# Moving the squaring of the hidden units and the residual's gain to other places in VectorE's order of an fp32 MLP

## What is computed

```
def squared_relu_mlp(x, w1, w2):
    h = jax.nn.relu(x @ w1)          # (256, 2048) @ (2048, 8192)
    return (h * h) @ w2              # (256, 8192) @ (8192, 2048)

x = layer_norm(ALPHA * x + mix, ln_mix_g[layer], ln_mix_b[layer])
x = layer_norm(ALPHA * x + squared_relu_mlp(x, mlp_w1[layer], mlp_w2[layer]), ln_mlp_g[layer], ln_mlp_b[layer])
```

## Time and profile before

| | |
|---|---|
| time, median of 3 runs | 2160.62 us (2160.14 to 2162.01) |
| the profiled execution: its time, its span | 2162.01 us, 2159.9 us |
| TensorE busy | 2131.8 us, 99% of the span |
| VectorE busy | 1423.9 us, 66% |
| ScalarE busy | 990.5 us, 46% |
| granted TensorE clock, mean | 0.997 |
| chain that ended last, by engine | PE 97%, DVE 1%, DMA 1% |

### The profile page before, as it was taken

How to read it: one execution, slowest core, us unless ns; L and a number is a source line. 1 busy time by engine, 2 the same in 40 slices (tenths; PEclk the granted TensorE clock), 3 DMA queues, 4 the chain that set the end, 5 groups by cost and what they waited for, 6 DMA issues and landing times.

```text
span 2159.9 us, 27393 instructions
## 1 busy us (share of the span) xinstructions
PE 2131.8 (99%) x10034; PEld 1786.6 (83%) x10034; DVE 1423.9 (66%) x1448; ACT 990.5 (46%) x1160; POOL 28.4 (1%) x38
## 2 busy tenths in 40 slices
PE   8999999999999999999999999999999999999997
PEld 7888888888888888888888888888888888888886
DVE  5866766766666666666787666567666666566667
ACT  4545656444444444444645554554444444444442
POOL 2000000000000000000000000000000000000002
PEclk9999999999999999999999999999999999999998
DMA  9554565666666666665564555456666666666662
GB/s 281 176 176 156 174 235 166 225 226 201 204 194 224 204 200 196 216 202 196 186 218 155 191 175 175 176 158 210 224 217 202 201 203 209 204 203 207 201 213 106
DMA packets 244767, 425.83 MB, mean 197 GB/s; under 512 B 14992, under 2 KB 50048, under 8 KB 243696
## 3 DMA queue, kind: packets, MB, share of 16 engines
q1 hardware_dynamic: 242880, 415.75, 59.5%
q0 software_dynamic: 1840, 9.44, 1.3%
HBM read 406.26 MB, written 2.10 MB: 189 GB/s over the span
## 4 chain that ended last, share of the span: by engine, by line
PE 97%; DVE 1%; DMA 1%; ACT 0%; SPq 0%; issue 0%
PE ps L714 26%; PE ps L716 26%; PE ps L715 26%; PE ps L688 11%; PE ps L692 5%; DMA raw<-in_ev_w_in 1%; PE ps L789 0%; PE ps L754 0%; PE ps L830 0%; PE ps L734 0%; PE ps L733 0%; PE ps L732 0%; PE ps L788 0%; PE ps L793 0%; DVE res L1125 0%; DVE stats L1091 0%
## 5 line engine op out<-in xcount | busy, mean ns | idle before, releaser
L380 ACT ACTIVATE w_hi<-raw 128x1024 fp32r<-128x1024 f32 x752 | 794.1, 1060 | 951.0 <-PE ps L716 888.7
L1005 DVE TENSOR_TENSOR w_lo<-raw,w_hi 128x1024 fp32r<-128x1024 f32 x752 | 901.4, 1218 | 302.6 <-ACT w_hi L380 302.4
L714 PE MATMUL ps<-w_hi,yT 128*128 128x512 f32 x1240 | 483.8, 390 | 0.0
L716 PE MATMUL ps<-w_hi,yT 128*128 128x512 f32 x1240 | 482.5, 389 | 0.0
L715 PE MATMUL ps<-w_lo,yT 128*128 128x512 f32 x1240 | 482.4, 389 | 0.0
L714 PE MATMUL ps<-w_hi,xT 128*128 128x512 f32 x1216 | 475.3, 391 | 2.1 <-DVE xT L1035 2.1
L716 PE MATMUL ps<-w_hi,xT 128*128 128x512 f32 x1216 | 473.3, 389 | 0.0
L715 PE MATMUL ps<-w_lo,xT 128*128 128x512 f32 x1216 | 473.2, 389 | 0.0
L1077 DVE TENSOR_TENSOR res<-ps,res 128x1024 f32<-128x1024 f32 x131 | 160.3, 1224 | 225.6 <-PE ps L716 225.6
L715 PEld LDWEIGHTS ps<-w_lo,yT 128*128 128x128 f32 x1240 | 232.8, 188 | 48.2
L716 PEld LDWEIGHTS ps<-w_hi,yT 128*128 128x128 f32 x1240 | 232.8, 188 | 48.3
(11 more groups left out here) (181 smaller groups left out, 775.1 us busy)
## 6 DMA issues: line engine op xcount, KB each, us to landing
raw<-in_mlp_w SPq DMA_DIRECT2D x256, 1024.0 KB, 5.3
raw<-in_od_w_in SPq DMA_DIRECT2D x48, 1024.0 KB, 5.2
raw<-in_ev_w_in SPq DMA_DIRECT2D x36, 1024.0 KB, 5.1
raw<-in_ev_w_out SPq DMA_DIRECT2D x16, 1024.0 KB, 5.1
ks<-cross SPq DMA_DIRECT2D x512, 32.0 KB, 1.9
raw<-in_od_w_out SPq DMA_DIRECT2D x16, 1024.0 KB, 5.0
raw<-in_ev_w_in SPq DMA_DIRECT2D x8, 512.0 KB, 13.1
res<-in_x SPq DMA_DIRECT2D x8, 256.0 KB, 9.7
```

Of the source, the lines that this page charges most:

```text
L380: nc.scalar.activation(flat(w_hi[:, k % NSPL]), flat(raw[:, k % NRAW]), ACT.Copy).then_inc(s_hi, 1)
L714: nc.tensor.matmul(bank, src[:, kt + i, 0, toks], hi, start=(start and i == 0), stop=False)
L716: ins = nc.tensor.matmul(bank, src[:, kt + i, 1, toks], hi, start=False, stop=(stop and i == CK - 1))
L1005: nc.vector.tensor_tensor(flat(w_lo[:, k % NSPL]), flat(raw[:, k % NRAW]), flat(w_hi[:, k % NSPL]).bitcast(F32), ALU.subtract).then_inc(s_ ...
```

## The change

Five events get other places. On DVE and ACT the squaring and both halves of the split of the hidden values stand two chunks earlier, in each iteration (`squared` from after chunk 6 to after chunk 4, `hidden_hi` and `hidden_lo` from 7 to 5) and for the extra group of the last one (14 to 12 and 15 to 13). The four `gain_residual` of iteration 0 stand later, at 6, 8, 12, 14 in place of 2, 3, 10, 12. No instruction is added or removed.

```diff
@@ ScalarE, up_down
                     for k in range(2, 18):
                         split_hi(blk, k)
-                        if k == 7:
+                        if k == 5:
                             hidden_hi(i + h0)
-                        if k == 15 and last:
+                        if k == 13 and last:
                             hidden_hi(i + h0 + 1, hT_last)
@@ VectorE, up_down
                     for k in range(2, 18):
                         split_lo(blk, k)
-                        if k == 6:
+                        if k == 4:
                             squared(i)
-                        if k == 7:
+                        if k == 5:
                             hidden_lo(i)
                         if k == 9:
                             blocks_turned(blk, 0)
-                        if first and k in (2, 3, 10, 12):
-                            gain_residual(n, (2, 3, 10, 12).index(k))
-                        if k == 14 and last:
+                        if first and k in (6, 8, 12, 14):
+                            gain_residual(n, (6, 8, 12, 14).index(k))
+                        if k == 12 and last:
                             squared(i + 1)
-                        if k == 15 and last:
+                        if k == 13 and last:
                             hidden_lo(i + 1, hT_last)
```

## The result

The changed kernel takes 2172.85 us (median of 4 runs, 2172.32 to 2174.73) against 2160.51 for the kernel before on the same chip (2160.14 to 2162.01): 12.3 us more, ratio 1.0063, 95% interval 1.005 to 1.0077. The profiled execution took 2174.45 us with a span of 2172.3, 12.4 above that of before. Seven more executions of the changed kernel are on record beside these four, the profiled one among them: over all eleven the median is 2174.65 (2172.32 to 2176.41), 14 us over the kernel before.

The account below looks back on a forecast made before the run. TensorE, busy for 99% of the span, bounds the kernel. Stalls of 11.6 us, iteration 1's 0.3 and the clock's 1.3 make 13.2: 2175.2 from the profiled 2162.01, or 2173.8 as a median, range 2169.5 to 2179.

Parts of the forecast that it names:

- The wait behind chunk 4: Middle iterations: VectorE waits 5.1 us for the moves; chunk 5 keeps 0.6 us of slack, so TensorE loses nothing.
- Rival B: Middle iterations stall too: each of 28 loses 0.4 to 0.5 us, 13 us more, 2187; chance 0.07.
- Iteration 0: Chunk 5 of each MLP's iteration 0 waits for its late split: TensorE stands 3.18 us, then 1.99.
- Chunk 7, 0.44 each: In iteration 0 of each MLP, a gain_residual ahead of chunk 7's split adds 0.44 us.
- Last iteration: The extra squaring delays chunk 13 by 2.01 us; with chunk 14, 2.77 us in the first MLP and 2.79 in the second.
- Iteration 1: Later gains delay the end of iteration 0 on VectorE, so TensorE loses 0.1 to 0.2 us, twice: 0.3.
- I take it as drained: GpSimd's later 2 MB gain and bias load was assumed finished by iteration 1's last move issue, at 433.9.
- The clock: One fall to 1.2 GHz after the first 3.18 us stand, costing 1.6 to 1.9 us, net 1.3.
- The signs: TensorE waits four times by 2 to 3.2 us and twice by 0.4 to 0.8; VectorE waits in nearly all 32 squarings.
- A: The wait is hidden in full everywhere: no change, 2160.6 us; chance 0.05.
- C: Spreading the gains quickens the MLPs' 6144 matmuls by 0.8 ns each: 4.9 us faster, 2155.7; chance 0.03.
- D: Only iteration 0 or only the last stalls, by a shorter run of moves: 2167 us; chance 0.05.

Follow-up runs that it names:

- the loop alone: Only iterations 1 to 13 of each MLP have the squaring after chunk 4 and split after chunk 5, against the kernel before: 2161.52 against 2161.71 us.
- one chunk further: Only iterations 1 to 13 changed, squaring after chunk 3 and split after chunk 4, against the kernel before: 2231.32 against 2161.93 us.
- that edit alone: Only the last iteration's extra squaring and split moved, from 14 and 15 to 12 and 13, against the kernel before: 2166.76 against 2161.71 us.
- the two kernels with a filled pause: Changed kernel with 24 or 11 small identity matmuls ahead of chunk 5 in the first MLP's iteration 0: 2175.69 and 2173.74 us.
- moves that land sooner: Changed kernel with half of each group's 16 moves issued by GpSimd: 2167.32 against 2161.93 us for the kernel before.
- gains: Only the four gain_residual moved, to 6, 8, 12, 14, against the kernel before: 2161.57 against 2161.71 us.

## Why the prediction was right, and where a term was off

The forecast was 2173.8 with 2169.5 to 2179; measured 2172.85, and 2174.65 over all eleven executions. By its steps:

- *TensorE is the bound and a chunk takes 2.72 us.* Held: nothing of the change made it faster, and the spacing stayed wherever the operands were there.
- *The wait behind chunk 4 is 5.1 us and is covered in the middle with 0.6 to spare.* 5.08 us, 0.68 to spare, and no loss (0.9999 for the loop alone). Rival B, the middle iterations stalling, is out; one chunk further it is true and costs 69 us.
- *Iteration 0: 3.18 and 1.99.* 3.20 and 1.98. *Chunk 7, 0.44 each:* 0.52 in the second MLP; in the first, none, since the slow matmuls ahead of it left VectorE the time.
- *Last iteration: 2.01, in all 2.77 and 2.79.* 2.00 at chunk 13 in both, 0.82 and 0.81 at chunk 14. The sum of waits is 2.8 in both, the starts of the weight loads fall back by 2.65 in each, and it is 5.05 us for the two MLPs by the time of that edit alone: behind a pause the first two weight loads stand 0.11 apart in place of 0.23, so a wait costs about 0.1 less than it reads.
- *Iteration 1: 0.1 to 0.2, twice.* Mis-sized: 0.60 and 0.67. The step that failed is "I take it as drained". With the later load of gain and bias issued 5 us ahead of the moves, the last move landed 2.2 us after its issue, not 1.9; with the load held back, both waits were 0.4 us shorter. What is left, 0.2, is what the prediction had from VectorE's order. How much the load delays the moves differs from execution to execution: in the two kernels with a filled pause, the last moves of the second MLP's iteration 1 landed after 1.9 us in spite of it, and the waits were 0.38 and 0.47.
- *The clock: one fall after the first pause, net 1.3.* It fell there in this profile: chunk 5 took 4.2 us, where one behind a pause without a fall takes 2.6, so 1.6 more, and with the 0.5 saved at chunk 7 net 1.1. That it fell is in part luck, as two other traces show a pause of the same size without it. The Trainium skill, TensorE: Matmul & The Clock Gate, section HAM oscillation, has the fall paid anew at each pause that brings the clock down. With pauses of 2.1 us, 9 of 26 did.
- *The signs.* The prediction names six waits of TensorE, "some 12 us in all"; its own sum has eight and two more in iteration 1. The trace has nine.
- *Rivals A, C, D.* A: no. C: no. D, a shorter run of moves, did appear in the size of the pause: in the second trace of the changed kernel the first run of moves takes 10.80 us in place of 11.43, and the pause is 2.6 us.

The waits sum to 12.6 us and the clock to 1.6; less 0.1 for each of nine waits, and less the 0.96 that this execution was ahead at its start, that is 12.3, against 12.4 between both spans. The chain is shown: moves that land sooner take all of the waits away, and the parts alone give 0 (gains), 0 (loop) and 5 us (last). Iterations 0 weren't changed alone; in the changed kernel's trace the starts of the weight loads fall back by 4.7 and 2.3 us there, and by 0.5 and 0.6 in iterations 1. What stays open is when a pause brings the clock down.

## What to carry to other kernels

In a kernel bound by one engine, the slack of an instruction on another is its due time less its earliest start; moving a wait ahead in an in-order queue spends the slack of all that stands behind it. The price is zero until the margin is gone and then the whole rest each time: 26 waits of 5.1 us on VectorE were free at k = 4; 26 of 6.7 us at k = 3 cost 2.1 each, and 9 of them a slower clock on top. Work the special iterations out by themselves, the first and the last, since a gate that sits early in the steady loop sits late there.

## What was not expected of the hardware

A pause of TensorE doesn't always bring the clock down: pauses of 3.24, 2.68 and 2.62 us were followed by a granted clock of 0.50, those of 3.14, 2.59 and 2.57 weren't, nor were those of 2.0 in the changed kernel, while 9 of 26 of 2.1 to 2.3 us were. And 256 small transfers issued by GpSimd in place of SyncE left 6 us between the landing of the last store and the end of the span, in both kernels that had them. A load of 2 MB issued some 5 us ahead of a run of small moves made the last of them land 2.2 to 3.7 us after its issue in place of 1.9 (first MLP, four traces; in the second it was 1.9 to 2.4).
